# Working the expert tiles of a two-block network two at a time

## The reference

```
t = h.reshape(512, 1024)
# router: one of 4 groups, then 2 of its 4 experts -> gates[t, 16], zero but for two experts of each token
a = einsum('td,edf->tef', t, w1)        # w1, w3: 16 experts, 1024 x 256
c = einsum('td,edf->tef', t, w3)
act = silu(a) * c * gates[:, :, None]
y = einsum('tef,efd->td', act, w2)      # w2: 16 experts, 256 x 1024
```

## Time and profile before

| what | us |
|---|---|
| median of 3 timed runs (2746.37 to 2746.92) | 2746.53 |
| the profiled execution's own time | 2741.5 |
| its span (first to last instruction) | 2739.5 |
| PE busy in the span | 2681.4 |
| DVE busy | 1772.4 |
| POOL busy | 1597.1 |
| ACT busy | 1090.2 |

### The profile page before, as it was taken

One profiled execution on the slowest core, in us unless ns is written; L12 is line 12 of the kernel. 1 busy time (PEld: TensorE's weight loads), 2 busy tenths in 40 slices (PEclk: granted clock), 3 DMA queues, 4 the chain that ended last, 5 costly groups with the idle time before them and its releaser, 6 DMA issues. The chain is left out here.

```text
span 2739.5 us, 35274 instructions
## 1 busy us (share of the span) xinstructions
PE 2681.4 (98%) x12337; PEld 2093.5 (76%) x12337; DVE 1772.4 (65%) x2575; ACT 1090.2 (40%) x1892; POOL 1597.1 (58%) x979
## 2 busy tenths in 40 slices
PE   8999999999999999999999989999999999999998
PEld 6777778888887777788888877778777677787675
DVE  6787755444127787654444749886777588777775
ACT  3844423222025544432221011644556415545554
POOL 5754466666676744486666765576236555772263
PEclk9999999999999999999999989999999999999999
DMA  4332222333332312223333322236896232357951
GB/s 156 86 84 62 63 86 83 96 96 100 92 93 85 100 62 70 62 85 94 98 97 126 109 90 85 70 100 241 303 354 209 69 97 73 94 209 295 352 181 64
DMA packets 89673, 340.29 MB, mean 124 GB/s; under 512 B 21568, under 2 KB 24384, under 8 KB 80064
## 3 DMA queue, kind: packets, MB, share of 16 engines
q1 hardware_dynamic: 66592, 298.02, 32.9%
q0 software_dynamic: 19008, 26.28, 3.7%
q10 hardware_dynamic: 3936, 14.16, 1.4%
HBM read 368.77 MB, written 33.55 MB: 147 GB/s over the span
## 5 line engine op out<-in xcount | busy, mean ns | idle before, releaser
L188 POOL TENSOR_TENSOR wl<-ring,wh 128x1024 fp32r<-128x1024 f32 x317 | 784.0, 2473 | 26.4
L186 POOL TENSOR_SCALAR wh<-ring 128x1024 fp32r<-128x1024 f32 x317 | 352.0, 1111 | 724.1 <-PE ps L265 516.5
L263 PE MATMUL ps<-xh,wh 128*128 128x512 f32 x1592 | 633.8, 398 | 14.0 <-DVE xl L1421 11.8
L264 PE MATMUL ps<-xl,wh 128*128 128x512 f32 x1592 | 621.2, 390 | 0.0
L265 PE MATMUL ps<-xh,wl 128*128 128x512 f32 x1592 | 621.2, 390 | 0.0
L263 PEld LDWEIGHTS ps<-xh,wh 128*128 128x128 f32 x1592 | 299.6, 188 | 94.2 <-issue 12.6
L265 PEld LDWEIGHTS ps<-xh,wl 128*128 128x128 f32 x1592 | 299.6, 188 | 64.2
L264 PEld LDWEIGHTS ps<-xl,wh 128*128 128x128 f32 x1592 | 300.0, 188 | 60.8 <-issue 1.0
L1673 DVE SCALAR_TENSOR_TENSOR taps<-ps,par,taps 128x511 f32<-128x511 f32 x192 | 143.8, 749 | 232.1 <-ACT taps L1391 216.3
L3271 DVE TENSOR_TENSOR ew_l<-ew,ew_h 128x1024 fp32r<-128x1024 f32 x184 | 214.1, 1217 | 5.2 <-ACT ew_h L2794 5.1
L2794 ACT ACTIVATE ew_h<-ew 128x1024 fp32r<-128x1024 f32 x184 | 180.6, 1050 | 13.3 <-DMA ew<-in_eu 9.3
(11 more groups left out here) (628 smaller groups left out, 5326.0 us busy)
## 6 DMA issues: line engine op xcount, KB each, us to landing
ring<-in_w SPq DMA_DIRECT2D x343, 512.0 KB, 3.6
ew<-in_eu SPq DMA_DIRECT2D x32, 2048.0 KB, 12.5
ew<-in_ed SPq DMA_DIRECT2D x32, 1024.0 KB, 11.4
xrows<-xr ACTq DMA_DIRECT2D x8, 512.0 KB, 2.8
yrows<-xr ACTq DMA_DIRECT2D x8, 512.0 KB, 3.8
yg<-yrows SPq DMA_DIRECT2D x8, 512.0 KB, 5.1
z<-in_x SPq DMA_DIRECT2D x4, 512.0 KB, 5.7
join_in<-in_ln ACTq DMA_DIRECT2D x1, 2048.0 KB, 9.4
```

What stands on the lines that cost most here:

```text
L186: nc.gpsimd.tensor_scalar(hi, raw, 1.0, 0.0, ALU.mult, ALU.add).then_inc(sem["w_hi"], 1)
L188: nc.gpsimd.tensor_tensor(lo, raw, hi, ALU.subtract).then_inc(sem["w_split"], 1)
L263: nc.tensor.matmul(out, wh, xh, start=first, stop=False, **kw)
L264: nc.tensor.matmul(out, wh, xl, start=False, stop=False, **kw)
```

## The change

From tile 6 (`TWINS`) on the tiles are taken in pairs (j, j + 1) with j = 6, 8, ..., 20, eight pairs in each layer; tile 22 stays alone. On PE a pair is: both up groups, the turned hidden tiles of j - 1 and j in one bank with one copy for both, the row transposes of j + 2 and j + 3, and both down groups. The second of two turned tiles has its own banks (2 and 7) and buffers, the down matmuls of an even tile go to banks 0 and 1, and there are two `hact` buffers. In the last round before the pairs (j = 5) PE turns the rows of tile 7 right behind those of tile 6. ACT, DVE, SP and POOL follow in the same order. POOL keeps `gather_rows(j + 3)`, `scatter_rows(j - 1)` for j below 6, and puts `gather_rows(9)` behind them; in a pair it issues both gathers (j + 4, j + 5) and then both scatters.

PE, before and after:

```diff
-                    for j in range(TILES):
+                    for j in range(TWINS):
                         expert_up(j)
                         if j:
                             turn_hidden(j - 1)
-                        if j and j + 1 < TILES:
                             turn_rows(j + 1)
-                        if j:
+                            if j == TWINS - 1:
+                                turn_rows(j + 2)
                             expert_down(j - 1)
+                    for j in range(TWINS, TILES - 1, 2):
+                        expert_up(j)
+                        expert_up(j + 1)
+                        turn_hidden(j - 1, j)
+                        turn_rows(j + 2)
+                        if j + 3 < TILES:
+                            turn_rows(j + 3)
+                        expert_down(j - 1)
+                        expert_down(j)
+                    expert_up(TILES - 1)
+                    turn_hidden(TILES - 2)
+                    expert_down(TILES - 2)
```

POOL (the spare tiles' weights left out):

```diff
-                    for j in range(TILES):
...
-                        if j + 3 < TILES:
-                            gather_rows(j + 3)
...
-                        if j:
-                            scatter_rows(j - 1)
+                    for j in range(TWINS):
+                        gather_rows(j + 3)
+                        if j:
+                            scatter_rows(j - 1)
+                    gather_rows(TWINS + 3)
+                    for j in range(TWINS, TILES - 1, 2):
...
+                        for i in (j, j + 1):
+                            if i + 4 < TILES:
+                                gather_rows(i + 4)
+                        for i in (j - 1, j):
...
+                            scatter_rows(i)
+                    scatter_rows(TILES - 2)
```

ACT and DVE in a pair, and behind the last pair (waits left out):

```diff
+ACT                 for j in range(TWINS, TILES - 1, 2):
+                        if j > TWINS:
+                            y_evac(j - 2)
+                        weights_high(j + 1, (UP_PARTS - 1,))
+                        gate_silu(j)
+                        weights_high(j + 2, range(UP_PARTS))
+                        gate_silu(j + 1)
+                        turn_evac(j + 2)
+                        if j + 3 < TILES:
+                            turn_evac(j + 3)
+                        y_evac(j - 1)
+                        if j + 3 < TILES:
+                            weights_high(j + 3, range(UP_PARTS - 1))
+DVE                 for j in range(TWINS, TILES - 1, 2):
+                        if j > TWINS:
+                            y_evac(j - 2)
+                        weights_low(j + 1, (UP_PARTS - 1,))
+                        gated_hidden(j)
+                        if j == Z_AT + C8:
+                            spread_last()
+                        weights_low(j + 2, range(UP_PARTS - 1))
+                        scaled_token(j)
+                        hidden_evac(j - 1, j)
+                        gated_hidden(j + 1)
+                        turn_evac(j + 2)
+                        if j + 3 < TILES:
+                            turn_evac(j + 3)
+                        weights_low(j + 2, (UP_PARTS - 1,))
+                        y_evac(j - 1)
+                        if j + 3 < TILES:
+                            weights_low(j + 3, range(UP_PARTS - 1))
+                        scaled_token(j + 1)
+                    y_evac(TILES - 3)
+                    gated_hidden(TILES - 1)
+                    hidden_evac(TILES - 2)
+                    y_evac(TILES - 2)
                     hidden_evac(TILES - 1)
```

More of the change, by code:

```diff
@@ L1708 @@
 HI_SLOTS = 7
+TWINS = 6
 V_POOL = 0
@@ L1737, in turns_of, with is_twin, turns_until @@
     return len(range(k, n, of))
+def is_twin(j):
+    return TWINS <= j < TILES - 1 and j % 2 == 0
+def turns_until(j):
+    return j + 1 if j < TWINS - 1 else j + 1 - (min(j, TILES - 3) - (TWINS - 1) + 1) // 2
 def held(j):
@@ L1884, in second_block, with turned_second, turn_bank, down_bank @@
         ident = con("ident")
-        def turn_bank(j):
-            return 0 if j else 4
+        def turned_second(j):
+            return 1 if j > TWINS and j % 2 else 0
+        def turn_bank(j, half):
+            if turned_second(j):
+                return 7 if half else 2
+            return half if j else 4 + half
+        def down_bank(j):
+            return 0 if is_twin(j) else 5
         def hy_unit(j):
@@ L1973, in _, with next_up @@
                         sp.dma_start(par[:, :], d_par[layer + 1:layer + 2].rearrange("a p n -> p (a n)")).then_inc(sem["par_in2"], 16)
-                    for j in range(EXPERTS - EW_BUFS + 1):
+                    def next_up(j):
                         if j + EW_BUFS < EXPERTS:
@@ L2520, in expert_up, with turn_hidden @@
                             mm.then_inc(sem["up_mm"], 1)
[L2522 to L2526, removed]
+                    def turn_hidden(*tiles):
+                        for i, j in enumerate(tiles):
+                            pe.wait_ge(sem["hact"], at("hact", j + 1))
+                            for f in range(EC):
+                                to = (EC * i + f) * P
+                                mm = T.transpose(ps[:, 4, to:to + P], hact_of[j % 2][:, f * P:f * P + P], ident)
                         mm.then_inc(sem["hactt_mm"], 1)
@@ L2543, in expert_down @@
                                 a_ = EW_UP + f * D + half * S
-                                mm = T.matmul(ps[:, 5 + half, :], hactT[:, f, :], ew[:, b, a_:a_ + S], start=(f == 0), stop=(f == EC - 1))
+                                mm = T.matmul(ps[:, down_bank(j) + half, :], hactT[:, EC * is_twin(j) + f, :], ew[:, b, a_:a_ + S],
+                                              start=(f == 0), stop=(f == EC - 1))
                             mm.then_inc(sem["dn_mm" if half else "dn_half"], 1)
-                    for j in range(TILES):
+                    for j in range(TWINS):
                         expert_up(j)
@@ L3292, in turn_evac, with hidden_evac, gated_hidden, scaled_token @@
                             dve.wait_ge(sem["xgt_hi"], at("xgt_hi", 2 * j + half + 1))
[L3293 to L3299, removed]
+                            high, low = (of[turned_second(j)][:, 4 * half:4 * half + 4, :] for of in (xgT_h_of, xgT_l_of))
+                            V.tensor_tensor(low, ps[:, turn_bank(j, half), :].rearrange("p (k t) -> p k t", t=P), high, ALU.subtract
+                                            ).then_inc(sem["xgt_lo"], 1)
+                    def hidden_evac(*tiles):
+                        n = EC * len(tiles)
+                        dve.wait_ge(sem["hactt_mm"], at("hactt_mm", turns_until(tiles[-1])))
+                        V.tensor_copy(hactT[:, 0:n, :], ps[:, 4, 0:n * P].rearrange("p (f t) -> p f t", t=P)).then_inc(sem["hactt"], 1)
+                    def gated_hidden(j):
+                        dve.wait_ge(sem["silu"], at("silu", j + 1))
+                        if j >= 2:
+                            dve.wait_ge(sem["hactt_mm"], at("hactt_mm", turns_until(j - 2)))
+                        V.scalar_tensor_tensor(hact_of[j % 2][:, :], sil[:, :], slot_gate[:, held(j):held(j) + 1], ps[:, 2 + j % 2, DE:2 * DE],
+                                               ALU.mult, ALU.mult).then_inc(sem["hact"], 1)
+                    def scaled_token(j):
+                        if Z_AT <= j < Z_AT + C8:
+                            k = j - Z_AT
+                            do(V.scalar_tensor_tensor(z[:, k, :], z[:, k, :], ALPHA - 1.0, spec[:, k, :], ALU.mult, ALU.add))
                     def y_evac(j):
@@ L3342, in _ @@
[L3342 to L3350, removed]
```

100 lines of the change are left out of this document (66 added, 34 removed).

## The result

The changed kernel takes 2759.06 us (median of 6 runs, 2755.59 to 2766.44), the kernel before 2746.45 beside it: ratio 1.0049, 95% interval 1.0036 to 1.0062. That is +12.6 us where +14.5 was forecast. Later runs of the unaltered kernel, each beside the kernel before, gave 1.0039 (1.0025 to 1.0053) and 1.0059 (1.0042 to 1.0076).

What follows compares the result with a forecast made beforehand. PE's own list was taken as the bound, with DMA engines at 0.96. Waits 11.4, clock 3.4 and tail 1.4, less switching 0.7 and hidden tiles 1.0, gave +14.5 on 2746.5: 2761.0 us, 8-in-10 range 2750.5 to 2770.

Steps and rivals of the forecast that it cites:

- The rows of tiles 7 and 9: Entry into the pairs, both layers: PE waits for these gathers 2.3, 3.3, 2.2 and 3.6 us, together +11.4 us.
- Rival D: Gathers share DMA engines with weight loads yet come in time, from 9.1 us down for tile 7: 2746.2 us; chance 0.05.
- B: Rival: only the rows of tile 7 are late, the gather of tile 9 is not: +4.2, 2750.7 us; chance 0.13.
- C: Rival: pairs starve on late weights, hidden copies or gathers, four pairs in each layer: +12 on top, 2773 us; chance 0.09.
- One sign that the prediction had named for C: Pairs 8 to 14 showing PE waiting for hidden copies or weights would mean the forecast is wrong.
- The clock: Half clock behind the two longer waits, for tile 9, 1.7 us each: +3.4 us, bounds 0 and 6.8.
- the reading by which all four waits bring the half clock: From the Trainium skill on long idle gaps: if it held for all four waits, 6.8 in place of 3.4 us.
- The tail: Layer end: DVE computes tile 22's gate before copying tile 21's hidden tile, so PE waits longer: +1.4 us for two layers.
- Switching: PE's changes of matmul kind: a pair takes 20.00 us against 20.04, over 16 pairs -0.7 us, bounds 0 and -1.6.
- The interval of 0.227: Spacing in us of the 24 matmul intervals of a pair's second up group, giving 5.45 us for that group.
- Late hidden tiles: Tiles 6 to 11: DVE's late hidden tile, 0.5 us a layer, is covered by two groups of row transposes: -1.0 us.
- The sum: 11.4 + 3.4 + 1.4 - 0.7 - 1.0 = +14.5 us, so a median of 2761.0 us; chance 0.71.

Runs made afterwards that it cites:

- e_pool: Changed kernel, but POOL issues the gather of tile 9 right behind tile 8's, ahead of the scatter of tile 4: 2751.61 us, ratio 1.0022 to the kernel before.
- e_late7: e_pool's edit on the changed kernel, and the rows of tile 7 turned behind the down group of tile 4: 2747.35 us, ratio 1.0001.
- e_third: Changed kernel with a third buffer for tile 7's gathered rows, so gathers of tiles 7 and 9 go out a round earlier: 2747.5 us, ratio 1.0005.
- the three executions: Profiled executions of the unaltered changed kernel: its first set of runs, e_again and e_again2; medians 2759.06, 2757.35 and 2762.06 us.
- e_again: The changed kernel run again, unaltered, for its own scatter: 2757.35 us, ratio 1.0039 to the kernel before.
- e_split: Changed kernel with POOL's split of next-layer weights moved behind the pair's gathers: 2761.82 us, ratio 1.0068, beside 2762.06 for the changed kernel.
- e_again2: The changed kernel run a third time, unaltered, for its own scatter: 2762.06 us, ratio 1.0059 to the kernel before.
- e_short: Changed kernel loading only an eighth of each weight of tiles 6 to 15, output not the reference's: 2748.96 us (one run), beside 2745.95 for the kernel before.
- e_fill: Changed kernel with 12 and 24 constant transposes on PE ahead of the turns of tiles 7 and 9: 2756.95 us, ratio 1.0038, beside 2757.35 for the changed kernel.
- e_best: e_late7 with tile 21's hidden copy ahead of tile 22's gate, `spread_last` behind the hidden copy, POOL's split behind the gathers: 2747.03 us, ratio 0.9997.

## Why the prediction was right

**The rows of tiles 7 and 9** (+11.4 forecast). Both mechanisms are shown: e_pool takes away the second wait and leaves the first, e_late7 and e_third take away both, in two unlike ways. The forecast was 2.3, 3.3, 2.2, 3.6; the three executions gave 3.36, 2.33, 1.47, 5.09, then 2.52, 0, 2.13, 2.22, then 1.96, 1.84, 1.97, 2.81. Their mean sum is 9.2: the step was oversized by 2 us. Nearly all of that is tile 9 in layer 1, forecast 3.3, mean 1.4: its gather was taken at the 11.6 of the earlier trace rows, and took 10.9, 8.5 and 10.4. Over all places a gather took from 13.7 down to less than 8.5 (e_again, layer 1: issued at 1998.67, its rows wanted at 2006.25 + 0.88, and no wait).

**Rival D.** Weights and gathers do share what decides: with an eighth of the weight traffic the same gather took 5.4 us and there was no wait. At the traffic that this kernel has, a gather was in time at one of twelve places (under 8.5 us), and at one of four in e_split, both times tile 9 in layer 1. So the rival's condition is met now and then for one tile, not for the kernel. B fell as well: the gather of tile 9 was late in 5 of 6 places (6 of 8 with e_split's). For C the traces show no wait on weights or rows in any later pair. One sign that the prediction had named for C is there, PE waiting for hidden copies in a pair from 8 to 14: the 0.66 us at the pair j = 10. Its cause is another than C's, as e_split shows.

**The clock** (+3.4). In the first profile the clock was at 0.50 for 3.4 us behind the waits of 3.36 and 2.33, and for 6.7 us, of which PE worked 4.0, at the one of 5.09: half of 10.8 is 5.4 us. In the other two it was 1.7 (behind 2.52) and 3.4 (behind 1.96 and 2.81). The mean is 3.5, and that it is so near the forecast's 3.4 is luck. The forecast charged the two waits for tile 9 and gave nothing to those for tile 7. In the traces the first wait of layer 1, for tile 7, brought the half clock every time (1.7 an execution), and the waits for tile 9 did in three of six places (mean 1.8). Idles of 1.96 to 2.33 went either way, so the reading by which all four waits bring the half clock is not borne out either.

**The tail** (+1.4): 1.11 - 0.52 = 0.59 in layer 1, about the same in layer 2 (1.10), +1.2. The order put back, the wait is 0.52 again.

**Switching** (-0.7). Of the new pair the row is e_split's timeline above: row transposes at 2025.69 and 2045.68, a pair apart, make 19.99 us, forecast 20.00, against 20.04. The interval of 0.227 that the forecast used for the second up group stands in none of its rows; with the 0.229 that it worked out, a pair would have been 20.05 and the gain nothing. The 19.99 bears the 0.227 out.

**Late hidden tiles** (-1.0). This step failed in layer 1. The prediction put the lateness down to DVE's own list, which a pair covers. There it became a wait of 0.66, since POOL's split now fell on DVE's low part. In layer 2, where POOL splits nothing, e_late7's stage is 233.2 against 233.6 though its tail costs 0.59: with 0.4 for switching, about 0.6 remains as a gain; that is a remainder, not a wait seen in the trace.

**The sum.** Over both stages the three executions took +19.1, +11.1 and +14.3 us, mean 14.8; the forecast had 14.5. The medians of the same three sets of runs lie 12.6, 12.0 and 16.4 us above the kernel before. For the second execution: waits 6.87, clock 1.7, a further stretch at 0.50 at the start of stage 1 (1.7), tail 1.2, hidden tiles 0.66, switching -0.7 make 11.4. That further stretch lies in time ahead of all that the change moves; it is also in the traces of e_again2, e_pool, e_third, e_short and e_fill, and not in those of before, after, e_split, e_late7 and e_best. Whether the change has a part in it stays open. The oversized waits, the missing gain on hidden tiles and this stretch cancel in part, so the sum is nearer than its terms. Outside the stages, in code that wasn't changed, one execution differs from another by more than some terms here: 2271.1 in the one profile of before, 2269.2 to 2280.5 in those of after.

## What to carry to other kernels

When a reordering asks for a transfer earlier, take the time at which its buffer came free and the duration of the same transfer in the same traffic, and do the subtraction for the first instances; the steady state may be fine and the entry into it not. Then look at what stands ahead of the next issue on its queue: a late result delays a scatter, and the gather behind it. Here, with DMA nearly full and PE too, a buffer more (e_third) or asking later (e_late7) gave the loss back, and filling the gap (e_fill) gave nothing that could be measured.

## What the runs showed of the hardware

VectorE's subtraction of two SBUF tensors did not slow down in proportion beside POOL's but seems to have stood until it ended: 3.31 and 2.79 us in place of 1.21, each ending 1.1 us behind POOL's end. One more in the changed kernel's trace, begun at 2073.86 beside a subtraction of 2.40 us on POOL, took 3.44 and also ended 1.1 behind it. The Trainium skill has this (SBUF — State Buffer, section SBUF: two separate sides): VectorE with two SBUF inputs and a GpSimd operation that reads SBUF lock one port pair for a whole instruction, and the other blocks. The traces agree in these three places.

Idle time of PE and the clock behind it, in the waits of over 1.4 us for gathers in the traces above: behind 1.47, 1.84 (twice), 1.97, 2.13 and 2.22 us it stayed at 1.00; behind 1.96, 2.12, 2.32, 2.33, 2.52, 2.65, 2.66, 2.81, 3.36 and 5.09 it fell to 0.50, in all but the last for 3.4 us. The nearest pair is in one execution, e_again2, in the windows behind 1.96 and behind 1.97:

```profile
1997.00:2000.00 3.00, 3.00 (x7) 1.50 (x6) 1.64 (x3) 1.08 (x2) 0.00 (x0) 0.50 0.92 384
2557.00:2560.00 3.00, 3.00 (x13) 1.85 (x14) 1.27 (x3) 1.27 (x3) 0.00 (x0) 1.00 1.02 401
```

So idle length alone doesn't decide near 2 us; what else does, these runs leave open.
